# The value products of two attentions move 64 columns instead of 128

## The reference

```python
# first block, per query block: 8 heads, value width 64
p = jax.nn.softmax(scores.astype(jnp.float32), axis=-1).astype(v.dtype)
return jnp.einsum('bhqk,bkhd->bqhd', p, v)
# second block: selected branch, window branch, DSA; value width 64
jnp.einsum('bgrqk,bgqkd->bgrqd', p.astype(vg.dtype), vg)
jnp.einsum('bgrqs,bsgd->bgrqd', p.astype(vv.dtype), vv)
jnp.einsum('bhqk,bqkd->bqhd', p.astype(vg.dtype), vg)
```

## Time and profile before

| | us |
|---|---|
| median of 3 runs | 2017.39 |
| lowest and highest | 2014.57, 2021.49 |
| the profiled execution, its own time | 2017.21 |
| its span in the trace | 2015.4 |
| PE busy | 1887.6 |
| DVE busy | 1194.0 |
| POOL busy | 1134.1 |

### The profile page before, as it was taken

How to read it: one execution, slowest core, us unless ns; L and a number is a source line. 1 busy time by engine, 2 the same in 40 slices (tenths; PEclk the granted TensorE clock), 3 DMA queues, 4 the chain that set the end, 5 groups by cost and what they waited for, 6 DMA issues and landing times.

```text
span 2015.4 us, 24841 instructions
## 1 busy us (share of the span) xinstructions
PE 1887.6 (94%) x8884; PEld 1502.7 (75%) x8884; DVE 1194.0 (59%) x1715; ACT 358.8 (18%) x743; POOL 1134.1 (56%) x1061
## 2 busy tenths in 40 slices
PE   6999999989999999899999987988889979999997
PEld 3788888868757888688888864666668748788785
DVE  7888468763854206688248637485785277306713
ACT  2100000021235211201000013101666120000001
POOL 3576777765650468577677682364100528767771
PEclk8999999999999999999999998897999989999998
DMA  8555455422320132455255341222000212323321
GB/s 285 180 195 167 154 181 199 162 89 66 98 78 1 42 105 84 159 179 177 84 197 167 115 114 29 63 65 84 22 1 2 63 38 87 105 89 99 102 86 42
DMA packets 223865, 214.38 MB, mean 106 GB/s; under 512 B 20210, under 2 KB 219055, under 8 KB 223791
## 3 DMA queue, kind: packets, MB, share of 16 engines
q1 hardware_dynamic: 222736, 212.75, 32.8%
q10 hardware_dynamic: 1054, 0.66, 0.1%
HBM read 211.30 MB, written 2.10 MB: 106 GB/s over the span
## 4 chain that ended last, share of the span: by engine, by line
PE 86%; DVE 10%; issue 2%; ACT 1%; POOL 1%; DMA 0%; ACTq 0%; DVEq 0%; POOLq 0%; SPq 0%
PE ps L623 24%; PE ps L625 24%; PE ps L624 24%; PE ps L1156 2%; PE ps L1136 1%; PE ps L1145 1%; DVE rb L1533 1%; PE ps L925 1%; PE ps L902 1%; PE ps L671 1%; DVE score L1928 1%; DVE blk_sum L1955 1%; PE ps L911 1%; DVE tt L2090 1%; DVE tt L1770 1%
## 5 line engine op out<-in xcount | busy, mean ns | idle before, releaser
L525 POOL TENSOR_TENSOR w_lo<-raw,w_hi 128x512 fp32r<-128x512 f32 (+2 forms) x604 | 785.9, 1331 | 12.6
L623 PE MATMUL ps<-h_hi,w_hi 128*128 128x512 f32 x1424 | 567.4, 398 | 33.5 <-DVE h_lo L1555 26.7
L624 PE MATMUL ps<-h_lo,w_hi 128*128 128x512 f32 x1424 | 559.9, 393 | 0.0
L625 PE MATMUL ps<-h_hi,w_lo 128*128 128x512 f32 x1424 | 559.8, 393 | 0.0
L518 POOL TENSOR_TENSOR w_hi<-raw,ones 128x8 fp32r<-128x8 f32 x151 | 34.2, 226 | 829.9 <-PE ps L625 780.5
L623 PEld LDWEIGHTS ps<-h_hi,w_hi 128*128 128x128 f32 x1424 | 270.9, 190 | 97.7 <-issue 34.2
L1562 DVE SCALAR_TENSOR_TENSOR ada_sum<-ada,cT,ada_sum 128x256 f32<-128x256 f32 x378 | 324.5, 859 | 13.4
L624 PEld LDWEIGHTS ps<-h_lo,w_hi 128*128 128x128 f32 x1424 | 270.8, 190 | 57.9 <-issue 1.9
L625 PEld LDWEIGHTS ps<-h_hi,w_lo 128*128 128x128 f32 x1424 | 270.5, 190 | 58.0
L623 PE MATMUL ps<-g_hi,w_hi 128*128 128x512 f32 x608 | 237.4, 390 | 3.2 <-ACT sg L1492 3.2
L625 PE MATMUL ps<-g_hi,w_lo 128*128 128x512 f32 x608 | 236.6, 389 | 0.0
(11 more groups left out here) (279 smaller groups left out, 2133.2 us busy)
## 6 DMA issues: line engine op xcount, KB each, us to landing
ada<-in_ada_w SPq DMA_DIRECT2D x31, 1024.0 KB, 5.2
ada<-in_w_ada SPq DMA_DIRECT2D x24, 1024.0 KB, 6.7
raw<-in_ffn_w_gate SPq DMA_DIRECT2D x22, 1024.0 KB, 6.8
raw<-in_ffn_w_up SPq DMA_DIRECT2D x22, 1024.0 KB, 5.1
raw<-in_w_in SPq DMA_DIRECT2D x16, 1024.0 KB, 5.0
raw<-in_w_up SPq DMA_DIRECT2D x16, 1024.0 KB, 5.3
raw<-in_w_down SPq DMA_DIRECT2D x16, 1024.0 KB, 5.0
raw<-in_ffn_w_down SPq DMA_DIRECT2D x16, 768.0 KB, 4.4
```

The costliest lines, as they stand in the source:

```text
L525: last = pool.tensor_tensor(lo[:, c], src[:, c], hi[:, c].bitcast(F32), ALU.subtract)
L623: pe.matmul(o, wh, xh, start=start, stop=False)
L624: pe.matmul(o, wh, xl, start=False, stop=False)
L625: return pe.matmul(o, wl, xh, start=False, stop=stop)
```

## The change

In both attentions the moving slice becomes the head's own 64 columns. The output of a query chunk is then 64 columns wide and lies at 64 times the chunk's number in the same bank; `at` goes, and VectorE reads 256 columns in one piece. The number of products, their order, their weights, the semaphores and every transfer stay as they are: on PE 4201 instructions stand in the same order in both kernels, and those of lines 925 and 1156 read 128x64 where they read 128x128.

```diff
-                     v=(lambda h, c: v_all[:, c, P * (h // 2):P * (h // 2) + P]), at=V_DIM * (h % 2), col=V_DIM * h,
+                     v=(lambda h, c: v_all[:, c, V_DIM * h:V_DIM * h + V_DIM]), col=V_DIM * h,
...
-                        v=(lambda c, b=b: v2[:, c, P * b:P * b + P]), at=HD * g, col=HD * h, added=sums))
+                        v=(lambda c, b=b, g=g: v2[:, c, P * b + HD * g:P * b + HD * g + HD]), col=HD * h, added=sums))
...
-                v=(lambda c: v2[:, c, 192:320]), at=HD, col=HD * (NSA_HEADS + 2 * j + g), added=0) for g in range(2)])
+                v=(lambda c: v2[:, c, 256:320]), col=HD * (NSA_HEADS + 2 * j + g), added=0) for g in range(2)])
...
-                    last = pe.matmul(ps[:, B_O[u % 2], P * qc:P * qc + P], pt[:, t % 2, P * c:P * c + P],
+                    last = pe.matmul(ps[:, B_O[u % 2], HD * qc:HD * qc + HD], pt[:, t % 2, P * c:P * c + P],
...
-                    last = pe.matmul(ps[:, B_O[side], P * qc:P * qc + P], pt2[:, t % 4, P * c:P * c + P], x["v"](c),
+                    last = pe.matmul(ps[:, B_O[side], HD * qc:HD * qc + HD], pt2[:, t % 4, P * c:P * c + P], x["v"](c),
...
-                src = ps[:, B_O[u % 2]].rearrange("p (q d) -> p q d", q=NQ)[:, :, x["at"]:x["at"] + HD]
+                src = ps[:, B_O[u % 2], 0:NQ * HD].rearrange("p (q d) -> p q d", q=NQ)
...
-            src = ps[:, B_O[side]].rearrange("p (q d) -> p q d", q=NQ)[:, :, x["at"]:x["at"] + HD]
+            src = ps[:, B_O[side], 0:NQ * HD].rearrange("p (q d) -> p q d", q=NQ)
```

## The result

The changed kernel is slower: 2030.44 us (median of 5 runs, 2028.9 to 2033.05) against 2015.97 (5 runs, 2014.57 to 2021.49), a ratio of 1.0068 with a 95% interval of [1.0051, 1.0085]. I had forecast 2012.9 and a range up to 2021. The profiled execution has a span of 2027.1 us against 2015.4. Both traces hold 8884 passes of TensorE.

A forecast was written before the change was run, and what follows sets the result against it. Both attentions were taken as bound by TensorE, the second together with VectorE for its first two thirds. Run ends give 2.5 + 3.4, less 1.6 for a clock fall: 4.3 us off 2017.2, so 2012.9 us, range 2006 to 2021.

The forecast's parts named there:

- I count one more fall: +1.6 us: Second attention's pauses: TensorE's clock falls to 1.2 GHz three times instead of two, costing 1.6 us; bounds 0 and seven others.
- rival B: Second attention's five fall-free pauses and both attentions' ends: seven more clock falls, 2022.5 us if short, 2033.7 if long; chance 0.12.
- My second ground: First attention: columns fill about 0.81 of the time afterwards, without pause, so the clock was expected to stay at 1.00.
- the steady stream of value passes gains nothing at all: Value products of both attentions: the weights' load sets the pace, so a 64-column pass still costs 0.111 to 0.112 us.
- rival A: Value products of both attentions: the move sets the pace and every pass halves, giving 1981.6 us; chance 0.05.
- What the ends give back: Ends of value-pass runs: 2.5 us back in the first attention and 3.4 us in the second.
- my own sign of being wrong on the ends: First attention: the forecast is wrong on the ends if a step stays at 2.19 us instead of 2.11.
- My value 0.03 for the trailing: First attention: scores behind a value run trail their load by 0.03 instead of 0.11 us, so start 0.08 us earlier.
- 0.10 a run: Second attention: runs going over into scores or VectorE's division end 0.10 us sooner, 28 x 0.10 of the 3.4 us.
- my lower bound of 1.4: Second attention's run ends: only the last pass's shorter move comes back, 28 x 0.05 = 1.4 us.
- no fall would be added: Clock by the skill's idle-gap rule: no gap grows by more than 0.1 us, so the sum would be 1.6 us lower.
- Rival C: Run ends of both attentions: nothing comes back, or PE's gain becomes waiting for DVE or ACT; about 2017 us, chance 0.25.

The follow-up runs named there:

- h1: Changed kernel with three unread products of 256 columns ahead of the scores of step 32 alone, in the last pause: 2019.93 us, ratio 1.002.
- h2: Changed kernel with three unread products of 256 columns ahead of the scores of step 36 alone, behind the last pause: 2030.7 us, ratio 1.0061.
- e5: Kernel before, with the second attention's value products moving 96 columns and the first attention unchanged: 2020.76 us, ratio 1.0012.
- e6: Kernel before, with the second attention's value products moving 32 columns, so half its result is not computed: 2048.64 us, ratio 1.0126.
- f1: Changed kernel with three unread products of 256 columns ahead of the scores at each of seven pauses: 2014.35 us, ratio 0.9994.
- e1: Kernel before, with only the first attention's value products moving 64 columns: 2016.48 us, ratio 0.9991.
- e4: Kernel before, with 64 columns in the last four pairs of the second attention alone: 2016.7 us, ratio 0.9999.
- f2: Changed kernel with the 21 added products at the seven pauses moving 1 column each instead of 256: 2030.93 us, ratio 1.0072.

## Why the prediction was wrong

It failed at one step, "I count one more fall: +1.6 us". In its place came two more falls and longer ones: 41 us of the stage at half clock instead of 6.8, 17.1 us of full-clock time, of which the stage shows +14.1. The rest of the sum was small and mis-sized, but it would have left the time in the range.

**The clock.** My rival B was the mechanism, and its direction and place were right: the pauses of the second attention. Its size was not. I priced a fall as an event of fixed length, 1.6 or 3.2 us, that TensorE leaves by itself. By those prices two more falls, even long ones, cost 6.4 us at most. In the changed kernel two falls are twice as long as those of before, and the one behind the last pause covers 24 us of dense work. That 2030.4 lies between B's 2022.5 and 2033.7 is luck: B reached such a time with seven more falls, not with two. The rows to see it were there: a run of 8 value passes took 1.47 us at half clock, and I had worked out that a load sets the pace; a stretch of such passes has nothing in it that moves more per microsecond at half clock than at full clock. That this is why it does not recover is an argument. What the runs show are two parts. Wide passes in the pause keep the long fall from starting (h1 against the changed kernel, with the same falls ahead of it), and wide passes behind the pause end it (two of the three profiles of h2, 17.1 us instead of 23.9). With e5 and e6 the fall behind the last pause also goes by width, 3.4 us with 128 and with 96 columns, 24 with 64, 55 with 32, one profile each for 96 and 32. What they leave open is why four of eight profiles with 64 columns have no long fall at that pause at all. My second ground, that the moved columns fill 0.81 of a step of the first attention without harm, held: its clock stayed at 1.00. It just does not carry over to a stage with pauses.

The price per fall is about right once its length is known: 17.1 us of full-clock time lost in the changed kernel gave +14.1, and in f1 the 3.4 regained and the gain at the runs' ends gave -2.9 together.

**The pace of a pass.** Right: "the steady stream of value passes gains nothing at all". The starts are 0.112 us apart with 64 columns as with 128, all but the first distance of a run; rival A (1981.6 us) is dead. The rule on the gap from the columns alone in the Trainium skill ("TensorE: Matmul & The Clock Gate", Back-to-back issue gap), which the page gives for a matmul taken by itself, does not hold in this stream; its addition that the load sets the spacing too does.

**What the ends give back.** Mis-sized. First attention: 2.5 us forecast, 0.4 measured (0.3 in e1, 73.4 us): the run is 0.05 shorter, and the next two passes lose 0.05, so the step stays at 2.19 us, my own sign of being wrong on the ends. My value 0.03 for the trailing came from a product of another kind (line 623) and did not hold for line 902. Second attention: 0.10 a run forecast, 0.05 measured; scores still start 0.205 us behind the start of the last value pass, with 64 columns as with 128, where I had expected 0.15. For the four last pairs e4 gives 0.6 us. So 3.4 us were rather 1.5 to 2, an estimate from these two, just above my lower bound of 1.4.

**Idle gaps.** I wrote that by the Trainium skill ("TensorE: Matmul & The Clock Gate", Why this matters for your kernels) no fall would be added. Here that misled: the seven waits grew by no more than 0.06 us and falls were added (one more wait, of 0.64 us, lies behind the last; h1 has it too, 0.66 us, and no fall there), and f2, whose passes of one column make the gaps shorter, leaves the clock at 0.87.

**The rest.** VectorE has 103.5 us of work in the stage in both kernels; its read in one piece costs and gives nothing that shows. Rival C had the first attention's time right, but not by its reasons: the trailing distance did change, and the chain of a step is still all TensorE's.

## What to carry to other kernels

Before you cut the moved columns of products whose weights' load sets the pace, expect next to nothing beyond the run's ends, and ask what the clock will do: near pauses the columns that look wasted may be what holds TensorE at 2.4 GHz, as they were here. Do not price a fall of the clock by the length of the falls in the profile at hand; here it was 3.4 us before and up to 24 us after, over work of the same list. Where a pause is set by another engine and falls follow it, try a product of wide columns into free PSUM: in this kernel three of them fitted into each long pause, with a wait of 0.26 to 0.53 us left, and the clock held; with one column each it did not. And profile a kernel more than once before you read a cause from a fall that is absent: which pauses have one can differ between executions of the same kernel.

## What the runs showed of the hardware

- With 128 weights' columns in float32 a pass starts every 0.112 us for 1, 32, 64, 96 and 128 moved columns (f2, e6, the changed kernel, e5, the kernel before); at half clock every 0.213 us (64 and 32).
- Half clock over dense work lasted 24 us where the value passes moved 64 columns (TensorE busy for 23.36 of 24.00) and 54 us where they moved 32 (53.85 of 54.00). With 96 or 128 columns no such stretch was seen in the second attention.
- The clock falls behind the same pause in one execution and not in another: of eight profiles with the same code up to there, four have the long fall and four have none.
- A change from products over 128 rows to products over 64 takes 0.205 us at full clock from the last start to the next first one, with 64 moved columns as with 128; I had read it as the move plus 0.1.
